# Hybrid attention, retention and state-space trunk: a new order at the head of each layer, another bank for weighted values, re-centring on VectorE

## What is computed

```python
h = rms_norm(x, norm_mix_g[l])
aq, ak, av, rq, rk, rv, rg, sz, sxbc, sdt = split(h @ w_in[l])
ya = swa_sink_attention(aq, ak, av, sinks, attn_bias)   # 8 heads, window of two chunks
yr = retention(rq, rk, rv, rg, gn_g)                    # 4 heads, values of width 128
ys = ssd_mixer(sz, sxbc, sdt, ...)                      # causal conv, softplus(dt), chunk scan
x = x + concatenate([ya, yr, ys]) @ w_out[l]
x = x + conv_ffn(rms_norm(x, norm_ffn_g[l]), ...)
```

## Time and profile before

| | |
|---|---|
| median of 3 runs | 1306.26 us (1304.59 to 1306.29) |
| the profiled execution | 1307.44 us |
| its span in the trace | 1305.6 us |
| TensorE matmul busy | 98% of the span |
| VectorE, ScalarE, GpSimd busy | 47%, 43%, 45% |
| mean granted TensorE clock | 0.996 of full speed |

### The profile page before, as it was taken

How to read it: one execution, slowest core, us unless ns; L and a number is a source line. 1 busy time by engine, 2 the same in 40 slices (tenths; PEclk the granted TensorE clock), 3 DMA queues, 4 the chain that set the end, 5 groups by cost and what they waited for, 6 DMA issues and landing times.

```text
span 1305.6 us, 21212 instructions
## 1 busy us (share of the span) xinstructions
PE 1277.4 (98%) x6114; PEld 1032.3 (79%) x6114; DVE 615.3 (47%) x938; ACT 565.3 (43%) x902; POOL 588.8 (45%) x435
## 2 busy tenths in 40 slices
...
DMA packets 77483, 125.29 MB, mean 96 GB/s; under 512 B 7752, under 2 KB 20456, under 8 KB 77288
## 3 DMA queue, kind: packets, MB, share of 16 engines
...
## 4 chain that ended last, share of the span: by engine, by line
PE 83%; DVE 8%; ACT 4%; issue 4%; DMA 0%; DVEq 0%; SPq 0%; ACTq 0%
PE dense L1048 76%; PE mix L1048 6%; DVE h_lo L690 1%; ACT w_hi L481 1%; DVE arena L991 1%; DVE ssq L698 1%; DVE arena L739 1%; ACT L525 1%; DVE arena L993 1%; ACT m_hi L498 0%; DMA x<-in_xT 0%; DVE arena L910 0%; ACT pad L525 0%; DVE mx L920 0%; DVE arena L926 0%
## 5 line engine op out<-in xcount | busy, mean ns | idle before, releaser
L378 POOL TENSOR_TENSOR w_lo<-w_raw,w_hi 128x512 fp32r<-128x512 f32 x424 | 580.3, 1384 | 686.8 <-ACT w_hi L481 680.1
L1048 PE MATMUL dense<-h_hi,w_hi 128*128 128x512 f32 x1120 | 445.3, 398 | 3.9 <-DVE h_lo L690 3.0
L1048 PE MATMUL dense<-h_lo,w_hi 128*128 128x512 f32 x1120 | 437.3, 390 | 0.0
L481 ACT ACTIVATE w_hi<-w_raw 128x512 fp32r<-128x512 f32 x422 | 256.3, 627 | 258.4 <-PE dense L1048 242.4
L1048 PE MATMUL dense<-h_hi,w_lo 128*128 128x512 f32 x1120 | 300.5, 389 | 0.0
L1048 PEld LDWEIGHTS dense<-h_hi,w_hi 128*128 128x128 f32 x1120 | 211.0, 188 | 55.3 <-issue 10.0
L1048 PEld LDWEIGHTS dense<-h_lo,w_hi 128*128 128x128 f32 x1120 | 211.0, 188 | 45.2 <-issue 2.7
L1048 PEld LDWEIGHTS dense<-h_hi,w_lo 128*128 128x128 f32 x1120 | 210.4, 188 | 44.4
L1048 PE MATMUL dense<-m_hi,w_hi 128*128 128x512 f32 x544 | 217.3, 400 | 3.2 <-ACT w_hi L481 2.5
L1048 PE MATMUL dense<-m_lo,w_hi 128*128 128x512 f32 x544 | 212.0, 390 | 0.0
L1048 PE MATMUL dense<-m_hi,w_lo 128*128 128x512 f32 x544 | 146.9, 389 | 0.0
...
## 6 DMA issues: line engine op xcount, KB each, us to landing
...
```

The source lines that it names most:

```text
L378: nc.gpsimd.tensor_tensor(w_lo[:, s, :], w_raw[:, s, :], w_hi[:, s, :].bitcast(f32), ALU.subtract).then_inc(lo_ready, 1)
L481: nc.scalar.activation(w_hi[:, slot, :], w_raw[:, slot, :], ACT.Copy).then_inc(hi_ready, 1)
L1048: return T.matmul(dst, lhsT, rhs, start=start, stop=stop)
```

## The change

The four U steps of PE become H (`group_high`: the products with the high weights, tiles 4 to 7), L (`group_low`: those with the low weights; L2 holds its high part too) and L3 (`group_last`). H0 and H1 stand ahead of NORM, and DT ahead of L0. On DVE and ACT the U steps stay, but U2 and U3 move behind D4 and D6; DX (DVE's share of DT), CR and CX (ACT's and DVE's shares of CM) become steps of their own, and CM and BC of PE stand behind D8. NORM moves to bank 1. ACT converts packs at other places. The gated weights `wdt_g` of DT are made by POOL instead of DVE. AV1 to AV3 use bank 5; AV0 stays in bank 0. RV is four plain transposes, and DVE, no longer ACT, empties the bank: sum over the 128 values, times 1/128, subtraction. All four squares of the retention's norm come at RN0; a step RM0 behind D36 holds the matmuls of tiles 2 and 3, all four Ln, two packs, then all four Exp; RN1 is gone. The constant `center` is gone.

```diff
+CONV_ORDER = (0, 1, 2, 5, 3, 7)
...
-    "G0 G1 G2 G3 NORM U0 DT U1 U2 TK U3 TT D4 DTB D5 DTC D6 D7 CM D8 BC TOL D9 SA0 D10 D11 SB0 SA1 D12 D13 SB1 SA2 D14 D15 "
+    "G0 G1 G2 G3 H0 H1 NORM DT L0 U0 DX L1 U1 L2 L3 TT TK D4 U2 DTB D5 D6 DTC U3 D7 CR CX D8 CM BC TOL D9 SA0 D10 D11 SB0 SA1 D12 D13 SB1 SA2 D14 D15 "
...
-    "RB0 RA1 D32 RB1 RA2 D33 RB2 RA3 D34 RB3 D35 RN0 D36 D37 RX0 D38 RX1 D39 RN1 D40 D41 RX2 D42 RX3 "
+    "RB0 RA1 D32 RB1 RA2 D33 RB2 RA3 D34 RB3 D35 RN0 D36 RM0 D37 RX0 D38 RX1 D39 D40 RX2 D41 RX3 D42 "
...
-    "NORM": (5,), "DT": (5,), "TK": (4,), "CM": (4, 5), "BC": (0, 2, 3), "SA": (0,), "SB": (1, 4, 5),
-    "AS": (0, 1, 4), "AT": (2, 3), "AV": (0,), "RP": (4,), "RV": (5,), "SN": (4,),
-    "RA": (0, 1, 2), "RB": (3, 4, 5), "RN": (0, 1),
+    "NORM": (1,), "DT": (5,), "TK": (4,), "CM": (4, 5), "BC": (0, 2, 3), "SA": (0,), "SB": (1, 4, 5),
+    "AS": (0, 1, 4), "AT": (2, 3), "AV0": (0,), "AV": (5,), "RP": (4,), "RV": (5,), "SN": (4,),
+    "RA": (0, 1, 2), "RB": (3, 4, 5), "RN": (0, 1), "RM": (2, 3),
 }
...
+    return BANKS[name] if name in BANKS else BANKS.get(step_of(name)[0], ())
...
-        rs2 = (ssq, rstd)
+        rs4 = (ssq[:, :], rstd[:, :], sq[:, 0, :], sq[:, 1, :])
+        sq4 = (sq[:, 0, :], sq[:, 1, :], pad[:, 0, 4:4 + S], pad[:, 1, 4:4 + S])
...
+            nc.gpsimd.memset(wdt_g[:, :, :], 0.0).then_inc(wdt_zero, 1)
...
+                nc.gpsimd.tensor_tensor(wdt_g[:, :, 0:8],
+                                        wdt_raw[:, bass.ds(l * 64, 64)].rearrange("p (k h) -> p k h", h=8),
+                                        par["g"][:, bass.ds(l * 2 * KD, KD)].unsqueeze(2).broadcast_to([P, KD, 8]),
+                                        ALU.mult).then_inc(wdt_ready, 1)
...
                         if n:
-                            hi_to(2 * GROUP + SLOTS - 1)
-                        if n == GROUP - 1:
-                            hi_to(2 * GROUP + SLOTS + 1)
+                            hi_to({1: 11, 2: 13, 3: 19}[n])
                         conv_silu(n)
...
                         if n in U_CONV:
+                            hi_to(2 * n + 7)
                             conv_silu(n)
...
-                    elif step == "CM":
-                        act.wait_ge(m_ready[5], ready(name, 1, l))
+                    elif step == "CR":
+                        hi_to(21)
+                        act.wait_ge(m_ready[5], ready("CM", 1, l))
                         nc.scalar.activation(crows[:, 0, :], M[5][:, 0:P], ACT.Copy).then_inc(rows_done, 1)
                         nc.scalar.activation(crows[:, 1, :], M[5][:, 0:P], ACT.Exp).then_inc(m_free[5], 1)
...
-                    elif step == "RV":
-                        act.wait_ge(m_ready[5], ready(name, 0, l))
-                        nc.scalar.activation(vtok[:, :, n, :], bank(5, 4), ACT.Copy).then_inc(m_free[5], 1)
...
+                        act.wait_ge(m_free[4], ready("RB3", 1, l) + 1)
+                        for t in range(4):
+                            nc.scalar.activation(sq4[t], ry[:, t, :], ACT.Square).then_inc(r_sq, 1)
+                    elif step == "RM":
+                        where = [("RN0", 0), ("RN0", 1), ("RM0", 0), ("RM0", 1)]
+                        for t, (name, i) in enumerate(where):
+                            act.wait_ge(m_ready[t], ready(name, i, l))
+                            nc.scalar.activation(rs4[t], M[t][:, :], ACT.Ln, scale=1.0 / P,
+                                                 bias=par["eps"][:, 0:1]).then_inc(m_free[t], 1)
+                        hi_to(packs[0] + 1)
+                        for t, (name, i) in enumerate(where):
+                            act.wait_ge(m_free[t], ready(name, i, l) + 1)
+                            nc.scalar.activation(rs4[t], rs4[t], ACT.Exp, scale=-0.5).then_inc(r_rs, 1)
...
+                    i = CONV_ORDER.index(n) % 2
...
-                    elif step == "DT":
-                        dve.wait_ge(m_ready[5], ready(name, 0, l))
+                    elif step == "DX":
+                        dve.wait_ge(m_ready[5], ready("DT", 0, l))
                         V.tensor_tensor(dts, M[5][:, :], rstd[:, :], ALU.mult).then_inc(m_free[5], 1)
...
-                    elif step == "CM":
-                        dve.wait_ge(m_ready[4], ready(name, 0, l))
+                    elif step == "CX":
+                        dve.wait_ge(m_ready[4], ready("CM", 0, l))
                         link(V.tensor_copy(tok[:, 32:64], M[4][:, 0:32]))
...
+                        av_bank = banks_of(name)[0]
...
-                            src = M[0][:, 256 * c:256 * c + 256].rearrange("p (t q) -> p t q", t=4)
...
-                                .then_inc(m_free[0] if c else a_lo, 1)
+                                .then_inc(m_free[av_bank] if c else a_lo, 1)
+                    elif step == "RV":
+                        dve.wait_ge(m_ready[5], ready(name, 0, l))
+                        link(V.tensor_reduce(vmean[:, :], bank(5, 4), AX.X, ALU.add))
+                        link(V.tensor_scalar(vmean[:, :], vmean[:, :], 1.0 / P, None, ALU.mult))
+                        V.tensor_tensor(vtok[:, :, n, :], bank(5, 4),
+                                        vmean[:, :].unsqueeze(2).broadcast_to([P, NB, P]),
+                                        ALU.subtract).then_inc(m_free[5], 1)
...
-                def group_unit(u):
+                def group_high(u):
 
                     for k in range(SLOTS, KD):
                         h_tile(l * 2)(k)
                         pe.wait_ge(hi_ready, l * N_PACKS + k + 1)
                         group_mm(u, k, False)
-                        if u == GROUP - 1:
-                            group_mm(u, k, True, stop=k == KD - 1).then_inc(run_done, 1)
-                    if u < GROUP - 1:
-                        for k in range(SLOTS, KD):
-                            pe.wait_ge(lo_ready, l * N_PACKS + k + 1 + SLOTS)
-                            ins = group_mm(u, k, True, stop=k == KD - 1)
-                        ins.then_inc(run_done, 1)
+
+                def group_low(u):
+
+                    for k in range(SLOTS, KD):
+                        pe.wait_ge(lo_ready, l * N_PACKS + k + 1 + SLOTS)
+                        ins = group_mm(u, k, True, stop=k == KD - 1)
+                    ins.then_inc(run_done, 1)
+
+                def group_last(u):
+
+                    for k in range(SLOTS, KD):
+                        group_mm(u, k, False)
+                        group_mm(u, k, True, stop=k == KD - 1).then_inc(run_done, 1)
...
+                    elif step == "H":
+                        group_high(n)
+                    elif step == "L":
+                        if n == GROUP - 1:
+                            group_last(n)
+                        else:
+                            if n == GROUP - 2:
+                                group_high(n)
+                            group_low(n)
...
-                            ins = mm(M[5][:, P * b:P * b + P], pad[:, (U_RV + n) % 2, at:at + BLK], center[:, :])
+                            ins = T.transpose(M[5][:, P * b:P * b + P], pad[:, (U_RV + n) % 2, at:at + BLK],
+                                              ident[:, :])
...
-                    elif step == "RN":
+                    elif step in ("RN", "RM"):
                         for j in range(2):
-                            pe.wait_ge(r_sq, l * 4 + 2 * n + j + 1)
+                            t = j if step == "RN" else 2 + j
+                            pe.wait_ge(r_sq, l * 4 + t + 1)
                             take(name, j, l)
-                            mm(M[j][:, :], ones[:, :], sq[:, j, :]).then_inc(m_ready[j], 1)
+                            mm(M[t][:, :], ones[:, :], sq4[t]).then_inc(m_ready[t], 1)
 
...
-N_CONST_LOADS = 2
+N_CONST_LOADS = 1
```

More of the change, by code:

```diff
@@ L96, with banks_of @@
 BANKS = {
[3 rows of a table removed]
-}
[3 rows of a table added]
+}
+def banks_of(name):
+    if name == "FNORM":
+        return BANKS["NORM"]
+    return BANKS[name] if name in BANKS else BANKS.get(step_of(name)[0], ())
 def bank_uses():
@@ L108, in bank_uses @@
         head, idx = step_of(name)
-        banks = (5,) if name == "FNORM" else BANKS.get(head, ())
+        banks = banks_of(name)
         for i, b in enumerate(banks):
@@ L121 @@
 ACT_LINKS = 5
-DVE_LINKS = 82
+DVE_LINKS = 90
 KB = 256
@@ L289, in ready @@
         def ready(name, i, l):
-            return l * BANK_TOTAL[BANKS_OF(name)[i]] + BANK_USE[(name, i)] + 1
+            return l * BANK_TOTAL[banks_of(name)[i]] + BANK_USE[(name, i)] + 1
         @block.sync
@@ L439, in rms @@
             def rms(e, name, l):
-                act.wait_ge(m_ready[5], ready(name, 0, l))
-                nc.scalar.activation(rstd[:, :], M[5][:, :], ACT.Ln, scale=1.0 / D,
-                                     bias=par["eps"][:, 0:1]).then_inc(m_free[5], 1)
-                act.wait_ge(m_free[5], ready(name, 0, l) + 1)
+                act.wait_ge(m_ready[1], ready(name, 0, l))
```

(29 more changed lines are left out.)

57 lines of the change are left out of this document (25 added, 32 removed).

## The result

The changed kernel takes 1318.60 us (median of 4 runs, 1318.11 to 1318.87), the kernel before 1306.28 us beside it (1304.59 to 1307.91): ratio 1.0094, with a 95% interval of 1.0077 to 1.0112. The prediction was 1300.0 us and faster; the kernel is slower by 12 us. The profiled execution's span is 1316.9 us, 11.3 us more than before.

A forecast was written before the change was run, and what follows sets the result against it. TensorE, busy 1277.4 of 1305.6 us, was taken as the bound. Head 4.3 plus D6's wait 0.45, minus 2 x 0.6 for the middle, plus 2 x 1.4 for the norm, gave about 6.3 us: 1300.0 us, range 1295.5 to 1304.5.

The forecast's parts named there:

- D6's wait: PE's wait for an evacuation in layer 1: goes, since D4 is evacuated ahead of U2; gain 0.45 us (0 to 0.5).
- The head: Layer start to D4: H0 and H1 fill the hole at NORM, no low clock; gain 4.3 us in layer 0, none in layer 1.
- The rows: Running sums' rows, with CM behind D8: cost 0, 3 to 4 us left before SB0, 2.5 us cover for packs behind SP.
- The low clock: TensorE's lower level behind a hole like NORM's: costs 1.7 us; not expected behind the remaining 0.8 us hole.
- rival D: AT1: a 3.4 us hole brings the low clock; middle loses about 4.5 us a layer; 1307.8 to 1309 us; 6%.
- RV and AT1: Attention's middle: transposes save PE 0.5 us eight times, AX1 ends 1.7 us later; with AV2, 0.6 us lost a layer.
- AV2: Bank 5 ends AV2's wait for bank 0, but the late copy of `pt` leaves a gain of 0.1 instead of 2.0 us.
- The retention's norm: D42 to D45: all Ln, then all Exp, so packs are no longer held up; gain 1.4 us a layer (0.8 to 2.1).
- B: Rival in the head: rows behind CM or a pack converted behind a silu come late; 1302.7 to 1304 us; 14%.
- E: Rival at RV: transposes replacing matmuls make the clock fall eight times, 1.7 us each; 1312 us; 1%.

The follow-up runs named there:

- e3: Changed kernel with ACT converting packs 22 and 23 ahead of SA0's two exps instead of behind them: 1306.94 us, ratio 1.0019.
- e5: Changed kernel with ACT writing the rows of the running sums ahead of D7's silu instead of behind it: 1303.40 us, ratio 0.9985.
- e1: Kernel before with the new order of the head alone: 1318.70 us, ratio 1.0099.
- e13: Changed kernel with NORM, L0 and U0 ahead of H1 and DT, and U2 ahead of D4: 1314.01 us, ratio 1.0068.
- e2: Kernel before with its own head and the other three parts (transposes with VectorE's re-centring, bank 5, retention's norm in one piece): 1307.53 us, ratio 1.0013.
- e10: Kernel before with only weighted values 1 to 3 in bank 5 and the retention's norm in one piece: 1301.08 us, ratio 0.9970.
- e4: Changed kernel with CM back ahead of D8 on PE: 1316.98 us, ratio 1.0088.
- e9: Changed kernel with NORM, L0 and U0 ahead of H1 and DT: 1317.79 us, ratio 1.0094.
- e14: Changed kernel with U2 ahead of D4 and nothing else: 1314.49 us, ratio 1.0076.

## Why the prediction was wrong

Its sum, step by step (us, after minus before, from the starts above; layer 0, layer 1):

| step | predicted | measured |
|---|---|---|
| head up to D4 | -4.3, 0 | -5.4, -0.1 |
| D4 to D10, with D6's wait | 0, -0.45 | +0.3, -0.3 |
| D10 to D12: rows, packs | 0, 0 | +7.2, +8.6 |
| D12 to D32: RV, AT1, AV2 | +0.6, +0.6 | +1.7, +1.8 |
| D32 to D45: the retention's norm | -1.4, -1.4 | -1.3, -1.3 |

**The head.** The mechanism held, and more: PE waited 0.37 us for pack 7 in place of 0.8 us, the clock stayed at 1.00 up to D4, and the sum of squares didn't hold NORM up.

**The rows, the failed step.** "Cost 0, SB0 has 3 to 4 us left" was wrong in two places, by 15.8 us in all with the low clock behind the waits. First, I asked who reads the rows and found SB0; I didn't ask what is queued behind the reader on its engine. Behind SA0's exps on ACT stand packs 22 and 23, wanted 5.5 us ahead of SB0. In layer 1 of the kernel before, D11 already came just as its pack was there (ACT converts at 720.33, D11 starts at 721.09): no slack, which I could have read. Second, I put the end of D7's convolution 3 us earlier in layer 0 and unchanged in layer 1, by adding up VectorE's queue at its old durations. D7's silu came 0.3 us later and 7.3 us later (2.5 of these handed on by layer 0): VectorE starts its chain 7 us ahead of D4 in place of 10.9 and 9.8, and its steps are longer beside POOL, so D7's last tap ends 32.8 us behind D4's start in both layers, in place of 27.1 and 28.0. So from D4 to D11 the layers need 5.4 and 6.0 us more, which in layer 0 swallows the head's gain and in layer 1, where there is none, is a plain loss. e3 and e5 show the queue, e1 that it is the head's alone; why the chain is as long as it is, is in part argued, as said at e13.

**The low clock.** The prediction priced it at 1.7 us and looked for it at NORM and, in rival D, at AT1. It came at D11, 2.0 and 2.3 us, and at AT1 in both layers: D21 to D24 loses 4.8 us, against 3.2 in e3, where the wait is as long and the clock stays up. Together some 7 us of the loss.

**RV and AT1.** The transposes saved less than priced: D12 to D21 holds all four units and gains 1.4 to 1.5 us, 0.36 a unit, where the prediction had 0.5 each. AX1's lateness was right, by parts that were off and made up for each other. It ends at 163.36 in place of 159.53, and 2.07 of these us were lost ahead of D12, so 1.8 are its own (1.8 in layer 1 too); predicted 1.7. VectorE in the changed kernel, to be read beside the earlier trace rows:

```profile
157.66 0.68 DVE L959 TENSOR_REDUCE vmean<-mix 128x4 f32<-128x512 f32 x1
158.37 0.54 DVE L960 TENSOR_SCALAR vmean<-vmean 128x4 f32<-128x4 f32 x1
158.95 0.69 DVE L961 TENSOR_TENSOR arena<-mix,vmean 128x512 f32<-128x512 f32 x1
...
161.24 2.12 DVE L944 TENSOR_TENSOR arena<-arena,den 128x1024 f32<-128x1024 f32 x1
...
163.42 1.09 PE L1305 MATMUL mix<-consts,arena 128*128 128x128 f32 x8 [3.15 <-DVE arena L944]
```

The three new steps cost 1.9 us and the last step of AX1 takes 2.12 in place of 1.23: 2.8 us in all, the prediction's upper end, where it had taken 2.4. The gate of D20, ahead of them, comes 1.0 us earlier within the layer (156.87 against 155.83, less the 2.07), where 0.7 was predicted. PE reaches AT1 1.4 us earlier, hence the wait of 3.15. AT1 itself starts 1.8 us late, as the sum had it. What the sum had at nothing is the lower clock behind that hole, 1.5 us a layer (28.1 us from D21 to D24 against 26.6 in e3). It stood in rival D alone, at 6%, and D's mechanism is what happened: a hole nearly as long as NORM's and the lower level behind it. D's price, 4.5 us a layer, did not: the middle lost 1.7 and 1.8. Without the new head, the other three parts leave the kernel within 0.2% of the one before (e2).

**AV2.** The prediction's gain of 0.1 us is the position at AV2 with AT1's wait in it. Read so, D12 to D25 loses 1.4 us in place of gaining 0.1: 1.5 gained by the transposes, 4.8 lost at AT1, 1.9 gained at AV2; the difference to the prediction is the clock's 1.5. The bank's wait itself went whole (e10: 1.8), since the copy is as late as PE is: done at 188.24, AV2 at 188.29. The later lag of VectorE was put at 0.7 and is 0.3 (D25 to D32); in e10 it is 0.7.

**The retention's norm.** Right: 1.25 us a layer against 1.4.

**The rivals.** B had the place ("a pack that ACT converts behind a silu come late", the rows) but a price of 2.7 us against 15.8, since I took it that half the head's gain could be lost and not that a chain could be longer than PE's own work. E (transposes pull the clock down) did not happen: PE's clock is 1.00 between D12 and AT1.

## What to carry to other kernels

When a step is moved, follow the data to its reader, and then the reader's queue to whatever is parked behind it: here two weight packs behind two exps turned the lateness of a side chain into a stop of the main engine, and moving either end of the chain by one step was worth 10 to 15 us. Gains ahead of a point count only if what is awaited there moves with them, so measure the distance from the gain to the next wait in both engines' queues, at the durations that the new neighbours leave. Compare times within a layer, from a common start: a step that looks late by its time in the trace may only have been handed the delay of an earlier stage. A cover found for one reader is no cover for the others.

## What the runs showed of the chip

Holes of the same length are followed by either level of TensorE's clock. The wait ahead of AT1 is 3.1 us in both layers of eight kernels (the changed one, e2, e3, e4, e5, e9, e13, e14), and the lower level follows in 8 of the 16 cases: in both layers of the changed kernel, e9 and e13, in one of e2 and e4, in none of e3, e5 and e14. Windows of e2: the stretch behind the hole in layer 0, then in layer 1.

```profile
159.80:161.50 1.70, 1.58 (x8) 1.32 (x8) 1.32 (x4) 0.34 (x1) 0.00 (x0) 0.62 0.57 154
...
799.80:802.00 2.20, 2.20 (x25) 1.91 (x26) 1.50 (x4) 0.63 (x1) 0.00 (x0) 1.00 0.32 113
```

So the clock's price behind a hole of 3 us is 0 or some 1.5 us, and a sum has to carry both. Behind the holes ahead of D11 of 4.3 us and more (11 cases, up to 6.8 us) the clock was at the lower level each time. Shorter ones are not safe either: the 1.88 us ahead of D12 in e3 was followed by the lower level, the 2.34 us at NORM in e10 and the 1.8 us at AV2 in the kernel before and in e1 were not. ACT's change of table costs its row and no more where it stood in a queue: the load of 1.28 us ends at 65.31 and the exp starts at 65.32 (e5).
